# Second products of the experts: weight halves of two feature tiles by four k-tiles instead of four by two

## The reference

```python
u = jnp.take(peer_u, expert, axis=0)                         # expert: 16 of 16384 for each token and head
act = jax.nn.gelu(jnp.einsum('chkd,cd->chk', u, zc))
v = jnp.take(peer_v, expert, axis=0)
w = (gate * act.astype(jnp.float32)).astype(zc.dtype)
return jnp.einsum('chk,chkd->cd', w, v).astype(zc.dtype)
```

## Time and profile before

| | |
|---|---|
| median of 3 runs | 3000.86 us (3000.12 to 3013.1) |
| profiled execution | 2999.78 us, span 2997.9 us |
| PE busy | 2981.9 us, 15908 matmuls |
| DVE, ACT, POOL busy | 2122.7, 1567.1, 947.9 us |
| DMA | 713.66 MB in 452089 packets |
| `peer_v` loads | 256 of 512 KB, each of 512 runs of 1 KB |

### The profile page before, as it was taken

The page is one execution under the profiler, slowest core; times in us unless marked ns, Lnnn a source line. Parts: engine busy times, 40 slices in busy tenths (PEclk is TensorE's granted clock), DMA queues, the critical chain, the costliest instruction groups (busy, mean ns, idle before and its releaser), DMA issues.

```text
span 2997.9 us, 41878 instructions
## 1 busy us (share of the span) xinstructions
PE 2981.9 (99%) x15908; PEld 2562.4 (85%) x15908; DVE 2122.7 (71%) x3064; ACT 1567.1 (52%) x2160; POOL 947.9 (32%) x728
## 2 busy tenths in 40 slices
PE   9999999999999999999999999999999999999999
PEld 7888888888888888888888788888888888888887
DVE  8957985555555678778886799897767855545554
ACT  7654454444454454444455656656566534434443
POOL 0023458888882066666631200000522000000000
PEclk9999999999999999999999999999999999999999
DMA  8788979999998799999996555555555565576665
GB/s 287 238 289 280 347 223 240 269 248 243 247 244 249 239 303 349 345 345 347 345 318 196 190 183 171 174 183 186 190 189 176 189 188 190 190 205 194 193 193 148
DMA packets 452089, 713.66 MB, mean 238 GB/s; under 512 B 66736, under 2 KB 341424, under 8 KB 449200
## 3 DMA queue, kind: packets, MB, share of 16 engines
q1 hardware_dynamic: 306144, 574.70, 60.3%
q10 hardware_dynamic: 94544, 102.49, 10.3%
q0 software_dynamic: 51200, 33.78, 5.7%
HBM read 674.02 MB, written 70.39 MB: 248 GB/s over the span
## 4 chain that ended last, share of the span: by engine, by line
PE 93%; DVE 3%; issue 2%; ACT 1%; DMA 1%; POOL 1%; SPq 0%; ACTq 0%; POOLq 0%; DVEq 0%
PE G L586 40%; PE G L590 20%; PE G L645 3%; PE G L643 3%; PE G L644 3%; PE M L643 3%; PE M L645 3%; PE M L644 3%; PE G L672 2%; PE M L672 2%; PE M L670 2%; PE G L670 2%; PE G L671 2%; PE M L671 2%; DVE lo L1366 1%
## 5 line engine op out<-in xcount | busy, mean ns | idle before, releaser
L586 PE MATMUL G<-ZA,hi 128*128 128x512 f32 x5098 | 1766.3, 395 | 3.8 <-DVE lo L1366 2.4
L1366 DVE TENSOR_TENSOR lo<-raw,hi 128x1024 fp32r<-128x1024 f32 x1088 | 1335.9, 1242 | 511.5 <-ACT hi L970 466.6
L970 ACT ACTIVATE hi<-raw 128x1024 fp32r<-128x1024 f32 x1088 | 1131.6, 1056 | 598.8 <-DMA raw<-in_pv 266.3
L590 PE MATMUL G<-ZA,lo 128*128 128x256 f32 x5114 | 1389.8, 278 | 0.0
L586 PEld LDWEIGHTS G<-ZA,hi 128*128 128x128 f32 x5098 | 943.8, 188 | 210.0 <-DVE lo L1366 2.9
L590 PEld LDWEIGHTS G<-ZA,lo 128*128 128x128 f32 x5114 | 961.4, 188 | 16.7
L2069 POOL DMA_INDIRECT g_scratch<-sel,IDX x256 | 435.1, 1700 | 113.8 <-issue 80.8
L977 ACT ACTIVATE tA<-G 128x256 f32<-128x256 f32 x367 | 139.6, 381 | 532.3 <-PE G L590 526.4
L1372 DVE TENSOR_TENSOR tS<-G,tA 128x256 f32<-128x256 f32 x336 | 141.3, 421 | 291.0 <-ACT tA L977 287.6
L2085 POOL DMA_INDIRECT vrow<-v_wide,IXV x128 | 165.5, 1293 | 230.6 <-PE G L590 136.7
L643 PE MATMUL G<-hi,ZB 128*128 128x512 f32 x512 | 199.4, 389 | 0.0
(11 more groups left out here) (368 smaller groups left out, 2748.9 us busy)
## 6 DMA issues: line engine op xcount, KB each, us to landing
raw<-in_pu SPq DMA_DIRECT2D x256, 512.0 KB
raw<-in_pv SPq DMA_DIRECT2D x256, 512.0 KB
raw<-in_w_in SPq DMA_DIRECT2D x192, 512.0 KB
raw<-in_w_up SPq DMA_DIRECT2D x128, 512.0 KB
raw<-in_w_down SPq DMA_DIRECT2D x128, 512.0 KB
v_wide<-in_pv ACTq DMA_DIRECT2D x64, 512.0 KB
raw<-in_w_out SPq DMA_DIRECT2D x32, 512.0 KB
raw<-in_wq SPq DMA_DIRECT2D x32, 512.0 KB
```

Of the source, the lines that this page charges most:

```text
L586: pe.matmul(G[:, 0:512], w, Z[:, k, :], start=first, stop=False, skip_group_check=True)
L590: m = pe.matmul(G[:, 0:256], lo[POS[u][p] % NRAW][:, k % 8, :], weights(u, p)[1][:, k, 0:256], start=False, stop=last, skip_group_check=True)
L970: act.activation(hi[w][:, :, :], raw[r][:, :].rearrange("p (k n) -> p k n", k=8), ACT.Copy).then_inc(s_hi, 1)
L1366: dve.tensor_tensor(lo[r][:, :, :], raw[r][:, :].rearrange("p (k n) -> p k n", k=8), hi[w][:, :, :].bitcast(F32), ALU.subtract).then_inc(s ...
```

## The change

A half of a "v" unit now holds 2 feature tiles by 4 k-tiles, so a run of the load is 512 numbers, 2 KB; the load has 256 runs instead of 512. The unit's two halves are the two pairs of feature tiles of one quarter, for the same four k-tiles. Each matmul still has 512 moving columns, and reads them as 2 buffers x 2 tiles x 128. For that the raw/lo buffers become one tensor, and so do the hi buffers. A unit waits for its second half (hence for both), runs its 24 (q = 3: 12) matmuls and then steps `s_mm` by 2. Since there are 7 hi buffers, 19 of the 128 units have their first half in hi buffer 6 and the second in buffer 0 (`FLIPPED`); these exchange their feature pairs and their raw buffers, so that the three operands agree in order.

```diff
+FLIPPED = [STAGE[u][0] == "v" and POS[u][0] % NW == NW - 1 for u in range(N)]
+def raw_slot(h):
+    u, p = HALVES[h]
+    return POS[u][0 if p else 1] % NRAW if FLIPPED[u] else h % NRAW
+def raw_before(h):
+    return next(w for w in range(h - NRAW - 1, h) if raw_slot(w) == raw_slot(h) and w // NRAW == h // NRAW - 1)
...
-                n = 2 * n + p
-                part = ins["pv"][4 * q:4 * q + 4, 2 * c + n // 4, :, 256 * (n % 4):256 * (n % 4) + 256]
-                return part.rearrange("q p f -> p q f"), ZB, range(2 * n, 2 * n + 2)
+                f = 4 * q + 2 * (1 - p if FLIPPED[u] else p)
+                part = ins["pv"][f:f + 2, 2 * c + n // 2, :, 512 * (n % 2):512 * (n % 2) + 512]
+                return part.rearrange("q p f -> p q f"), ZB, range(4 * n, 4 * n + 4)
...
-                    sp_.wait_ge(s_mm, h - NRAW + 1)
+                    sp_.wait_ge(s_mm, raw_before(h) + 1)
...
-                if q == 0:
-                    pe.wait_ge(s_za, 8 * c + n + 1)
-                weights_ready(POS[u][p])
+                weights_ready(POS[u][1])
+                whi = his[:, 0:NW:NW - 1, :, :] if FLIPPED[u] else his[:, POS[u][0] % NW:POS[u][0] % NW + 2, :, :]
+                wlo = los[:, POS[u][0] % NRAW:POS[u][0] % NRAW + 2, :, :]
+                whi, wlo = (w.rearrange("p s (q k) f -> p s q k f", k=4) for w in (whi, wlo))
-                for x in range(2):
+                for x in range(4):
+                    if q == 0 and x % 2 == 0:
+                        pe.wait_ge(s_za, 8 * c + 2 * n + x // 2 + 1)
...
-                        vhi, vlo = whi[:, :, x, :], wlo[:, :, x, :]
+                        vhi, vlo = whi[:, :, :, x, :], wlo[:, :, :, x, :]
...
-                m.then_inc(s_mm, 1)
+                m.then_inc(s_mm, 2)
```

More of the change, by code:

```diff
@@ L297, in region @@
             return out
-        wts = [region(4096, f"wts{i}", [(f"raw{i}", [128, HALF], F32)], [(f"lo{i}", [128, 8, 128], F32R)]) for i in range(NRAW)]
-        raw, lo = [wts[i][f"raw{i}"] for i in range(NRAW)], [wts[i][f"lo{i}"] for i in range(NRAW)]
-        hi = [sb(f"hi{i}", [128, 8, 128], F32R) for i in range(NW)]
+        wts = region(4096 * NRAW, "wts", [("raw", [128, NRAW, HALF], F32)], [("lo", [128, NRAW, 8, 128], F32R)])
+        raws, los, his = wts["raw"], wts["lo"], sb("hi", [128, NW, 8, 128], F32R)
+        raw, lo = [raws[:, i, :] for i in range(NRAW)], [los[:, i, :, :] for i in range(NRAW)]
+        hi = [his[:, i, :, :] for i in range(NW)]
         za = region(32768, "za_mem", [("ZA", [128, 16, 512], F32R)],
@@ L531, in sync_program @@
                 if h >= NRAW:
-                    sp_.wait_ge(s_mm, h - NRAW + 1)
-                r = raw[h % NRAW][:, :]
+                    sp_.wait_ge(s_mm, raw_before(h) + 1)
+                r = raw[raw_slot(h)]
                 if BY_TOKEN[u]:
-                    r = r.rearrange("p (q f) -> p q f", q=4)
-                sp_.dma_start(r, weights(u, p)[0]).then_inc(s_raw[h % NRAW], 16)
+                    r = r.rearrange("p (q f) -> p q f", q=2 if STAGE[u][0] == "v" else 4)
+                sp_.dma_start(r, weights(u, p)[0]).then_inc(s_raw[raw_slot(h)], 16)
             for n in range(8):
@@ L588, in rest @@
             def rest(u, p, n, k, G, last):
-                m = pe.matmul(G[:, 0:256], lo[POS[u][p] % NRAW][:, k % 8, :], weights(u, p)[1][:, k, 0:256], start=False,
+                m = pe.matmul(G[:, 0:256], lo[raw_slot(POS[u][p])][:, k % 8, :], weights(u, p)[1][:, k, 0:256], start=False,
                               stop=last, skip_group_check=True)
@@ L623, in half, with expert_unit @@
                     x += step
-            def expert_half(u, p):
+            def expert_unit(u):
                 i, c = STAGE[u][1:]
                 q, n = expert_part(i, c)
-                n = 2 * n + p
                 if c == 0 and n == 0 and q in (1, 2):
                     pe.wait_ge(s_join, BANK[VB[0]])
-                if q == 0:
-                    pe.wait_ge(s_za, 8 * c + n + 1)
-                weights_ready(POS[u][p])
-                whi = hi[POS[u][p] % NW][:, :, :].rearrange("p (q k) f -> p q k f", k=2)
-                wlo = lo[POS[u][p] % NRAW][:, :, :].rearrange("p (q k) f -> p q k f", k=2)
-                for x in range(2):
+                weights_ready(POS[u][1])
[5 more added lines that the diff above has]
+                        pe.wait_ge(s_za, 8 * c + 2 * n + x // 2 + 1)
                     for h, G in enumerate(VM[q]):
@@ L640, in expert_half @@
                             continue
-                        zhi, zlo = (ZB[:, 2 * n + x, at:at + 128] for at in (128 * h, 256 + 128 * h))
-                        vhi, vlo = whi[:, :, x, :], wlo[:, :, x, :]
+                        zhi, zlo = (ZB[:, 4 * n + x, at:at + 128] for at in (128 * h, 256 + 128 * h))
+                        vhi, vlo = whi[:, :, :, x, :], wlo[:, :, :, x, :]
                         pe.matmul(G[:, :], zhi, vhi, start=c == 0 and n == 0 and x == 0, stop=False, skip_group_check=True)
                         pe.matmul(G[:, :], zhi, vlo, start=False, stop=False, skip_group_check=True)
-                        m = pe.matmul(G[:, :], zlo, vhi, start=False, stop=c == 7 and n == 7 and x == 1, skip_group_check=True)
-                m.then_inc(s_mm, 1)
+                        m = pe.matmul(G[:, :], zlo, vhi, start=False, stop=c == 7 and n == 3 and x == 3, skip_group_check=True)
+                m.then_inc(s_mm, 2)
             def down_ready(u, p):
@@ L667, in down_product @@
                 whi = hi[POS[u][p] % NW][:, :, :].rearrange("p (q k) f -> p q k f", k=2)[:, :, x, :]
-                wlo = lo[POS[u][p] % NRAW][:, :, :].rearrange("p (q k) f -> p q k f", k=2)[:, :, x, :]
+                wlo = lo[raw_slot(POS[u][p])][:, :, :].rearrange("p (q k) f -> p q k f", k=2)[:, :, x, :]
                 zhi, zlo = (ZB[:, 2 * n + x, at:at + 128] for at in (128 * h, 256 + 128 * h))
@@ L749, in apart @@
                     pe.matmul(G[:, :], hi[POS[w][0] % NW][:, k, :], Z, start=k == 0, stop=False, skip_group_check=True)
-                    pe.matmul(G[:, 0:256], lo[POS[w][0] % NRAW][:, k, :], Z[:, 0:256], start=False, stop=False, skip_group_check=True)
+                    pe.matmul(G[:, 0:256], lo[raw_slot(POS[w][0])][:, k, :], Z[:, 0:256], start=False, stop=False, skip_group_check=True)
                 pe.wait_ge(s_zr, 2)
@@ L757, in apart @@
                     for k in range(APART):
-                        whi, wlo, Z = hi[POS[w][0] % NW][:, k, :], lo[POS[w][0] % NRAW][:, k, :], ZB[:, 2 + k, :]
+                        whi, wlo, Z = hi[POS[w][0] % NW][:, k, :], lo[raw_slot(POS[w][0])][:, k, :], ZB[:, 2 + k, :]
                         pe.matmul(P, whi, Z[:, 0:256], start=k == 0, stop=False, skip_group_check=True)
@@ L871, in tensor_program @@
                 elif STAGE[u][0] == "v":
-                    expert_half(u, 0)
-                    expert_half(u, 1)
+                    expert_unit(u)
                 elif u == N - 1:
@@ L965, in prep @@
             def prep(h):
-                r, w = h % NRAW, h % NW
+                r, w = raw_slot(h), h % NW
                 act.wait_ge(s_raw[r], 16 * (h // NRAW + 1))
@@ L969, in prep @@
                     act.wait_ge(s_mm, h - NW + 1)
-                act.activation(hi[w][:, :, :], raw[r][:, :].rearrange("p (k n) -> p k n", k=8), ACT.Copy).then_inc(s_hi, 1)
+                act.activation(hi[w][:, :, :], raw[r].rearrange("p (k n) -> p k n", k=8), ACT.Copy).then_inc(s_hi, 1)
             def low(u, n=0):
@@ L1363, in prep @@
             def prep(h):
-                r, w = h % NRAW, h % NW
+                r, w = raw_slot(h), h % NW
                 dve.wait_ge(s_hi, h + 1)
-                dve.tensor_tensor(lo[r][:, :, :], raw[r][:, :].rearrange("p (k n) -> p k n", k=8),
+                dve.tensor_tensor(lo[r][:, :, :], raw[r].rearrange("p (k n) -> p k n", k=8),
                                   hi[w][:, :, :].bitcast(F32), ALU.subtract).then_inc(s_lo, 1)
```

## The result

| | before | changed |
|---|---|---|
| median | 3001.13 us (20 runs) | 3012.11 us (20 runs) |
| ratio | | 1.0035, 95% interval 1.0026 to 1.0043 |
| profiled execution, span | 2999.78, 2997.9 us | 3011.83, 3010.0 us |

The change makes the kernel 10 to 11 us slower, where 1.4 us had been forecast. Some executions of nearly every version, 4 of the 20 before, take about 12 us longer than the rest at the same granted clock; the medians hardly move by them, and their cause is not known.

What follows compares the result with a forecast made beforehand. PE was taken as the bound, at 226.5 ns per matmul. Terms 0 + 0 + 0.5 - 0.5 + 1.4 gave +1.4 us, a median of about 3002.2 us, range 2996 to 3011, with no measurable change at 86%.

Steps and rivals of the forecast that it cites:

- What bounds the kernel: second products: PE bound by number of matmuls times 226.5 ns between starts; DMA engines full, but PE not feeling it.
- Matmuls, the read over two buffers: second products: count stays 2688, new read costs 0; rival: from 5.6 ns a matmul slower, 3018 at 6 ns, 4%.
- Waits and signals on PE: unit borders: 128 weight waits and 128 `s_mm` steps go, gain 0; rival that signals cost: 3.4 us back, 2999.
- Packets: SP's weight loads: 65536 packets fewer, 3.5% of engine time freed in the full window, one load landing in 4.2 us.
- Later release, earlier need: inside the stage: each half loses 2.72 (1.36) us of reserve; 0.5 us, bounds 0 and 10, removed by faster landing.
- the subtraction: inside the stage: 2.72 (1.36) us taken from each of 216 halves' reserves; two halves late, 0.5 us in sum.
- End of the stage: turns 2 and 3: later loads delay both turns, waits about 4.5 and 3.3 us; +1.4 us, bounds -1 and +3.
- the wait before turn 3 shorter than 3.77: end of the stage: sign to check in the profile; PE's wait before turn 3 expected at about 3.3 us.
- a later start has less of that stretch in it: behind turn 2's wait: later start meets less of the 0.51 clock stretch, put at 0.5 us back.
- reserve runs out: full stage: paired loads land 1.9 us later or more, PE waits for DVE lo; 3018 at 2 us; chance 6%.
- another case, late weights in the middle: inside the stage: upper bound of 10 us for the lost reserve, which set the range's upper end of 3011.

Runs made afterwards that it cites:

- The other order of the tail: kernel before, ACT and DVE do copies and late sums ahead of splits, half 625 ahead of sum 10, quarter 3's copies early; 2997.90 and 2997.76 us.

## Why the prediction was wrong

- *What bounds the kernel*: right. PE, with 226.5 ns a matmul; the reserve behind it was the question.
- *Matmuls, the read over two buffers*: right at 0. In the unit borders and the middle of the changed stage two starts are 0.22 to 0.23 us apart, as in the earlier trace rows; the mean of those that did not wait is 226.7 ns in both traces. That rival is refuted.
- *Waits and signals on PE*: right at 0. Before, with twice the signals, no start in the window of 426 us was late, so there was nothing to give back. By the Trainium skill's rule (TensorE: Matmul & The Clock Gate, "The cost: per-tile semaphore tail") it would have been an estimated 3.4 us; the trace does not agree. That the tail runs beside the next matmul is the prediction's reading, no run tested it.
- *Packets*: the count was right. The relief was underestimated: the engines' share fell by 7 points, forecast 3.5; a packet of SP's queue in the window takes 46 ns for 1 KB and 84 ns for 2 KB in the median. Landing at the end of the stage was right, 4.3 us against 4.2. In the full stage the loads take longer: where ACT waited, 8.4 and 8.1 us in the median for first and second halves before, 6.3 and 8.2 after. So the second half of a pair, which PE now waits for, gained nothing, and this is where the forecast had counted on faster landing.
- *Later release, earlier need*, inside the stage: forecast 0.5 us before relief and 0 behind it, measured 2.0 us in the window. The chain into the longest wait, at 1290.76 us, shows what the subtraction left out:

```profile
1276.68 8.03 DMA raw<-in_pv
...
1284.73 1.07 ACT hi L984
...
1286.97 1.22 DVE A L1679
1288.19 1.38 DVE vacc L1712 x2
1289.57 1.15 DVE lo L1380
...
1290.76 0.50 PE G L658
```

  The halves of a unit are now loaded and split as a pair, and DVE's other work (L1679, L1712) comes between them; the second half, which used to have half a unit more, is the late one. The 0.5 us that the sum took off again for faster landing did not come off. This term was too small by 1.5 to 2 us.
- *End of the stage*: this step failed. "The reserve is gone already" was said of turns 2 and 3, and the delay was worked out for these alone. The same three steps, load, split, copy, stand ahead of turns 0 and 1; there 7.4 us of chain met 5.44 us of PE's work, 2.0 us each. A wait list says where the reserve is below zero, not where it is zero; and the earlier trace rows count a second wait behind L702, the 0.19 us at turn 1. Turn 2 was forecast to wait "about 4.5", it waits 4.7. Turn 3 waits 4.0, not 3.3; here the prediction slipped in its own sum, for a turn 1.4 us later behind work that ends 1.3 us later waits 3.77 + 0.1 = 3.9 us. Its sign "the wait before turn 3 shorter than 3.77" was wrong by this slip; the +1.4 us was not touched by it.
- *The low clock*: "a later start has less of that stretch in it" was wrong. The stretch around turn 2 is 6.8 us at 0.50 instead of 3.4, and turn 1 has one of its own. A stretch of 3.4 us at half clock costs about 1.7 us. That one behind turn 1, with 2.0 us more of waiting, is the +3.6 us from turn 1 to 2.
- *The rivals*: "reserve runs out" asked for a landing 1.9 us later in the full stage; no median there came later by more than 0.1 us, and this was not the mechanism. The mechanism of the loss, a late issue that delays a turn, was in the forecast as *end of the stage*, but for one chain and at 1.4 us.

In sum, terms of 0 (middle) and 1.4 us (end) were 2.0 and 8.6 us. The measured 3012.11 us lie above the range, whose upper end of 3011 stood for another case, late weights in the middle; that it is so near is luck. The prediction held that less than 0.5% could not be told from no change; 20 runs of each told 0.35%.

That late signals bring the loss is shown: alone they bring 14 us. That they do it by the turns is shown too: with the copies ahead of the splits no loss is left that the interval tells, and with old halves in chunk 7 neither. A new layout with early signals was not run. Why a stretch of half clock is 3.4 us in one trace and 6.8 in another stays open.

## What to carry to other kernels

When a release moves to a coarser grain, list everything that stands in order behind the work that it releases, not only the consumer of that buffer, and compare each chain (issue, landing, splits, copy) with the work its waiter has meanwhile. A hand-over that shows no wait can have no reserve at all: look up the producer's end beside the consumer's start at every place of the same pattern, and compare the distance with one where the consumer did wait (0.15 us here). Freed DMA time was worth nothing to this core, whose matmuls never starved, except as reserve for what the same edit took away.

## What the runs showed of the hardware that was not expected

- Each wait of 2.1 to 6.9 us before a turn, in all traces, was with or followed by a stretch of half clock of 3.4, 6.8 or 10.2 us: with late signals, whose turn 2 waits 6.9 us, the window below is at 0.50 throughout. The length of the wait does not settle it. A wait of 2.0 us before turn 0 of the changed kernel had none, one of 2.09 us before turn 1 had 3.4 us. Before turn 2, 4.73 us in the changed kernel had 6.8 us, and 4.62 us with 1 KB runs had 3.4. The other order of the tail, the same kernel in two traces, had 6.8 us in one and none in the other, with no wait over 1.4 us there in either.

```profile
1670.50:1680.70 10.20, 5.46 (x17) 4.72 (x18) 5.81 (x8) 6.26 (x11) 1.70 (x3) 0.50 0.37 132
```

- The load of 512 KB with fewer rows, or fewer runs, landed 0.3 to 0.9 us earlier in the median at light traffic, but one load with runs of 2 KB and two with runs of 1 KB landed alike (4.3 and 4.2 us) in the changed kernel.
- In the full stage, at a DMA share of 1.04, the same load took about 8 us from issue to split, against 5.1 us near its end.
